# A fused transformer kernel: regrouping its feed-forward tiles into 6, 8 and 8, with the normalized activations written beside the first down product

## What is computed

```python
# first_block
h = rms_norm(x, norm_ffn_pre_g[l])
f = (jax.nn.silu(h @ w_gate[l]) * (h @ w_up[l])) @ w_down[l]
x = x + rms_norm(f, norm_ffn_post_g[l])
# second_block, before and after its mixers
x = x + 0.5 * swiglu(rmsnorm(x, ffn1_norm[l]), ffn1_w_gu[l], ffn1_w_down[l])
x = x + 0.5 * swiglu(rmsnorm(x, ffn2_norm[l]), ffn2_w_gu[l], ffn2_w_down[l])
return rmsnorm(x, final_norm)
```

## Time and profile before

| | us |
|---|---|
| median of 3 runs (1966.96 to 1967.85) | 1967.25 |
| the profiled execution | 1967.67 |
| its span, from the first to the last instruction | 1965.9 |
| TensorE matmuls busy | 1908.2 (97%) |
| VectorE busy | 1238.5 (63%) |
| ScalarE busy | 851.8 (43%) |
| POOL busy | 493.5 (25%) |

### The profile page before, as it was taken

One profiled execution on the slowest core, in us unless ns is written; L12 is line 12 of the kernel. 1 busy time (PEld: TensorE's weight loads), 2 busy tenths in 40 slices (PEclk: granted clock), 3 DMA queues, 4 the chain that ended last, 5 costly groups with the idle time before them and its releaser, 6 DMA issues. The chain is left out here.

```text
span 1965.9 us, 27808 instructions
## 1 busy us (share of the span) xinstructions
PE 1908.2 (97%) x10930; PEld 1612.4 (82%) x10930; DVE 1238.5 (63%) x1866; ACT 851.8 (43%) x1453; POOL 493.5 (25%) x419
## 2 busy tenths in 40 slices
PE   9999999997999999979999999999999997999998
PEld 7777788876899898768998988777887786899897
DVE  6677545378467465774674666887654457467465
ACT  5344433454244244442442456665543344244244
POOL 4110002115143231342332342222010025143230
PEclk9999999998999999989999999999999998999999
DMA  6122233331433233223343332222232231433223
GB/s 174 55 65 65 70 100 107 111 90 56 118 90 109 86 105 110 86 69 103 87 118 90 99 103 74 65 66 65 86 97 65 76 93 56 118 87 109 86 79 104
DMA packets 340788, 176.57 MB, mean 90 GB/s; under 512 B 6481, under 2 KB 339378, under 8 KB 340658
## 3 DMA queue, kind: packets, MB, share of 16 engines
q1 hardware_dynamic: 340658, 174.79, 30.7%
HBM read 172.67 MB, written 2.10 MB: 89 GB/s over the span
## 5 line engine op out<-in xcount | busy, mean ns | idle before, releaser
L1868 DVE TENSOR_TENSOR WL<-RAW,WH 128x1024 fp32r<-128x1024 f32 (+3 forms) x371 | 415.6, 1126 | 251.9 <-ACT WH L1577 248.7
L1577 ACT ACTIVATE WH<-RAW 128x1024 fp32r<-128x1024 f32 (+3 forms) x371 | 326.4, 886 | 384.3 <-PE ps L1336 329.9
L1332 PE MATMUL ps<-HH,WH 128*128 128x512 f32 x1152 | 461.5, 401 | 0.9 <-ACT HH L1624 0.9
L1336 PE MATMUL ps<-HL,WH 128*128 128x512 f32 x1152 | 449.7, 390 | 0.8 <-DVE HL L1950 0.8
L1334 PE MATMUL ps<-HH,WL 128*128 128x512 f32 x1152 | 449.2, 390 | 0.7 <-DVE WL L1868 0.7
L1332 PE MATMUL ps<-GH,WH 128*128 128x512 f32 x688 | 269.3, 391 | 0.0
L1336 PE MATMUL ps<-GL,WH 128*128 128x512 f32 x688 | 267.9, 389 | 0.0
L1334 PE MATMUL ps<-GH,WL 128*128 128x512 f32 x688 | 267.8, 389 | 0.0
L1332 PEld LDWEIGHTS ps<-HH,WH 128*128 128x128 f32 x1152 | 216.4, 188 | 53.3 <-issue 8.2
L1336 PEld LDWEIGHTS ps<-HL,WH 128*128 128x128 f32 x1152 | 216.3, 188 | 49.2 <-DVE HL L1950 2.1
L1334 PEld LDWEIGHTS ps<-HH,WL 128*128 128x128 f32 x1152 | 216.5, 188 | 48.0 <-issue 4.1
(11 more groups left out here) (251 smaller groups left out, 3062.3 us busy)
## 6 DMA issues: line engine op xcount, KB each, us to landing
RAW<-in_ffn_w_gu SPq DMA_DIRECT2D x88, 512.0 KB, 3.8
RAW<-in_w_in SPq DMA_DIRECT2D x67, 512.0 KB, 3.7
RAW<-in_ffn_w_down SPq DMA_DIRECT2D x32, 512.0 KB, 3.7
RAW<-in_w_gate SPq DMA_DIRECT2D x22, 512.0 KB, 3.9
RAW<-in_w_up SPq DMA_DIRECT2D x22, 512.0 KB, 3.8
RAW<-in_w_out SPq DMA_DIRECT2D x16, 512.0 KB, 3.9
RAW<-in_mem_w_kv SPq DMA_DIRECT2D x16, 512.0 KB, 3.8
RAW<-in_w_down SPq DMA_DIRECT2D x16, 512.0 KB, 3.7
```

Source lines behind the costliest of these rows:

```text
L1332: e.matmul(bk, wh, xh, start=k == 0, stop=False)
L1336: last = e.matmul(bk, wh, xl, start=False, stop=k == kt - 1)
L1577: e.activation(at.weight(n, "H"), at.raw(n), ACT.Copy).then_inc(*sg.inc("hi", n))
L1868: e.tensor_tensor(at.weight(n, "L"), at.raw(n), at.weight(n, "H").bitcast(F32), ALU.subtract).then_inc(*sg.inc("lo", n))
```

## The change

`THIRDS` becomes groups of 6, 8 and 8 tiles, `PAIRS` becomes none, (0, 3, 6), (0, 3, 6), and `MIX_AT` gets one more empty entry, so that `PLAIN` is 6: the whole first group is plain and works on unnormalized H. `place` handles one chunk; it is called ahead of each of the eight tiles of the first group's down product and waits for the last up product as a whole, and the signals by chunk go. The fifth tile's splits ahead are no longer put off. In `last_down` the first part has `nf - 4` chunks, four where there were two, and the second part four as before.

```diff
-THIRDS = ((0, 8), (8, 8), (16, 6))
+THIRDS = ((0, 6), (6, 8), (14, 8))
-MIX_AT = ((0,), (1,), (2,), (3,), ())
+MIX_AT = ((0,), (1,), (2,), (3,), (), ())
 PLAIN = len(MIX_AT)
-PAIRS = ((5,), (0, 3, 6), (0, 3))
+PAIRS = ((), (0, 3, 6), (0, 3, 6))
...
-    def place(self, gen):
-
-        n = len(self.weights) - 1
-        self.by_chunk.add(n)
-        for c in range(KD):
-            self.step("place", gen, c, ("mm", ("k", n, c) if c < KD - 1 else n))
-            self.tiles.give(("N", gen, c), ("xl", ("H", ("n", gen), c)), ("mixed", (gen, c % 4, 3)))
+    def place(self, gen, c, done):
+        self.step("place", gen, c, done)
+        self.tiles.give(("N", gen, c), ("xl", ("H", ("n", gen), c)), ("mixed", (gen, c % 4, 3)))
...
                 if f:
-                    mu, = self.mtiles([su], ("H", gen, 0), [bu], ahead=f < PLAIN - 1)
-                if f == PLAIN - 1:
-                    self.place(gen)
-                    self.ahead(len(self.weights))
+                    mu, = self.mtiles([su], ("H", gen, 0), [bu])
+                    done = mu
                 self.step("gate_up", key, mu, bu, ("gr", key))
...
             for mt in range(KD):
                 b = self.bank(("db", G, mt))
+                if n == 0:
+                    self.place(gen, mt, done)
                 mm, = self.mtiles([(down, f0, nf, mt * P)], ("G", G, 0), [b], ahead=False)
...
-            mm, = self.mtiles([(down, f0, 2, mt * P)], ("G", G, 0), [b])
+            mm, = self.mtiles([(down, f0, nf - 4, mt * P)], ("G", G, 0), [b])
...
-                    self.weigh((down, f0 + 2, nf - 2, mt * P, mt))
-                self.groups.append((n + mt, 1, ("G", G, 2), [b], slice(256 * h, 256 * h + 256), nf - 2))
-                for k in range(nf - 2):
+                    self.weigh((down, f0 + nf - 4, 4, mt * P, mt))
+                self.groups.append((n + mt, 1, ("G", G, nf - 4), [b], slice(256 * h, 256 * h + 256), 4))
+                for k in range(4):
```

## The result

The changed kernel takes **1922.5 us** (median of 4 runs, 1921.1 to 1923.6), beside 1967.1 for the kernel before: a ratio of 0.9772, with a 95% interval of 0.9755 to 0.9789. The forecast was 1922.3. A later repetition gave 1922.1, ratio 0.9767 (0.9753 to 0.9782). The profiled execution took 1921.05 with a span of 1919.3, 46.6 less than before; it is the fastest of the four.

What follows compares the result with a forecast made beforehand. TensorE, busy 97% of the span, was taken as the bound, losing time only where it waits or runs slowly. Terms -47.9 + 0.4 + 2.6 = -44.9 took 1967.67 to 1922.8, by median 1922.3 us; range 1917 to 1932.

Steps and rivals of the forecast that it cites:

- step 1: First pair of each feed-forward, moved behind six plain tiles and a down product, loses its excess: -47.9 us in all.
- The 12.3 us of slow matmuls: Part of the 47.9 us excess at the first pairs, put down to TensorE's lower clock after idling.
- Step 3: Place, moved from beside the waiting pair to ahead of each first-group down tile, fits under TensorE: 0.
- Step 2: First pair's weights, fetched behind a 33 us down, arrive in time: 0; bound 4.1 us late in each feed-forward.
- Step 4: First group's six-chunk down, behind a plain tile, waits for G of the last tile: +0.4 us; stage 33.07.
- Step 5: Third group's last pair, now at its tile 6, has a slower gate half: +2.6 us, bounds 0 and twice that.
- Step 6: Last down in parts, with four chunks a tile in the first part: 0, bounds twice 0.43 us either way.
- Step 7: Ring tiles: eight N tiles held through the first down still free tiles in time for the pair's sums: 0.
- Rival (a): In the first group's down, place and POOL's sums block each other; a smaller wait returns: 1931 to 1947 us, chance 0.12.
- (b): The excess belongs to a first pair as such and moves with it: 1967 us, no change, chance 0.02.
- (c): First group's down starves on every tile and TensorE's clock stays at the lower level: 2009 us, chance 0.02.

Runs made afterwards that it cites:

- first and fourth expectation: Kernel before with its first pair at tile 6, not 5, of the first group: 1953.2 us; kernel before with two chunks mixed in a tile: 1973.9 us.

## Why the prediction was right, and where its reasons were not

**The size of the gain (step 1) was right and its cause was half the story.** The -47.9 was read as a difference of stages, pair against pair, and that difference holds whatever the causes are: 10.07 in all three. The step and the analysis ahead of it put it down to the mix chain, the clock behind it and small waits. The runs show two things on the path, one behind the other. The chain (with the sums, which as fills save 23 us) makes TensorE wait first; the block of place, ahead of weight splits and gate_up on VectorE, holds the pair after that. Taking away the wait for NH alone is worth 1967 x (1 - 0.9914) = 17 us, not 48. The forecast missed the median by 0.2 us, and that is in part luck: the profiled execution, forecast at 1922.8, took 1921.05.

**The 12.3 us of slow matmuls** were a true reading of the clock and a false price: in two feed-forwards keeping TensorE busy held the clock at 1.00 and saved nothing. Where the next wait followed anyway, the slow matmuls only filled it.

**Step 3 (place moves, 0)** was right about the new place, and it missed the old one. It booked no gain for taking the block away from the pair. One run shows what the old place costs by itself: the block put back ahead of gate_up, with no sums beside it, costs 20 us. In another, the pair moved without place keeps 10.9 of its 15.6 us of excess, but part of that may be the sums'. My 3.3 us for its remainder in the first and fourth expectation came from adding up the small waits behind the gap in the earlier trace rows, which were small because the gap hid the block.

**Step 2** held: sums 18.6 us in, 19.2 forecast. **Step 4** held to the hundredth: 33.08 against 33.07. **Step 5** held as a sum, 2.4 against 2.6, and not one by one (0.27, 0.87, 1.23 against 0.98, 0.72, 0.86), so that the sum came out is partly chance. **Step 6** held: the first part takes 21.79 us, 96 matmuls at 0.227. **Step 7**: no first pair or down tile loses time, so no late tile reaches TensorE.

**Rival (a)** had the right mechanism and too high a price. VectorE and POOL in the first group's down of the changed kernel:

```profile
490.42 1.78 DVE L1883 TENSOR_TENSOR HL<-TS,HH 128x512 fp32r<-128x512 f32 x1
...
L1883 DVE TENSOR_TENSOR HL<-TS,HH x24: 678/684/1787, 475.7 to 1651.5; 128x512 fp32r<-128x512 f32 x24
```

This place subtraction starts 0.13 us after the first sum (490.29, 1.36 long) and ends at 492.20, 0.55 behind that sum's end; alone it takes 0.68. It stood for the rest of the sum. That agrees with the rule of the Trainium skill ("SBUF — State Buffer", "Who interferes with whom"). But most of the subtractions meet no sum (three of the eight in this stage take some 1.8 us), since the sums start only 18.6 us in: the median of the 24 is 0.684, and VectorE's work in the stage was 23.4 us, not 36. Rivals (b) and (c) did not come: no first pair lost anything, and no down tile starved.

## What to carry to other kernels

That a stage takes 25 us where its twin takes 10 gave a good price for the whole of what hinders it, and no evidence of what that is: the trace names the wait that comes first, and the waits behind it look small because it hides them. Before one cause is taken away alone, ask what stands in the same queue behind it. In this kernel helper work in a block belonged behind the instruction that feeds the next matmuls, and where a product of 33 us followed it needed no spreading.

## What was not expected

A lower TensorE clock can be free: in the first feed-forward, at 0.80 of full speed over 25.65 us before and at 1.00 with TensorE kept busy, the pair reached its sixth product at 483.19 and at 483.14. And the clock can fall on a short wait in one place and not in another: with the gap filled, a wait of 1.60 us ahead of the sixth product left it up in the first feed-forward and took it down in the third. Why was not found.

Two versions that each took away the longest wait (the pair one tile later, two chunks a trip) differ by 21 us, and the one that mixed earliest was the slower: what its weight splits lost behind the long trips on VectorE was more than the wait was worth.
